# Gathering the first expert's rows in the router's stage, with VectorE's and GpSimd's work around it put in another order

## The reference, cut to what matters

```python
def moe_swiglu(x, w_router, b_router, w1, w3, w2):
    ...
    logits = (xt @ w_router).astype(jnp.float32) + b_router.astype(jnp.float32)
    top_v, top_i = lax.top_k(logits, TOP_K)
    gates = jax.nn.softmax(top_v, axis=-1)
    dense_gate = jnp.sum(jax.nn.one_hot(top_i, N_EXPERTS, dtype=jnp.float32) * gates[..., None], axis=1)
    y = jnp.zeros_like(xt)
    for e in range(N_EXPERTS):
        y = y + dense_gate[:, e:e + 1].astype(x.dtype) * swiglu(xt, w1[e], w3[e], w2[e])
```

## Time and profile before

| | |
|---|---|
| time, median of 3 runs | 2537.49 us (2537.44 to 2538.87) |
| profiled execution: its own time | 2535.22 us |
| its span in the trace | 2533.3 us |
| PE, PEld busy | 2451.1 us (97%), 2023.4 us (80%) |
| DVE, ACT, POOL busy | 1753.3 us (69%), 1056.2 us (42%), 607.0 us (24%) |
| router's end to the first expert's first matmul | 1052.6 us to 1065.45 us |

### The profile page before, as it was taken

How to read it: one execution, slowest core, us unless ns; L and a number is a source line. 1 busy time by engine, 2 the same in 40 slices (tenths; PEclk the granted TensorE clock), 3 DMA queues, 4 the chain that set the end, 5 groups by cost and what they waited for, 6 DMA issues and landing times. The chain is left out here.

```text
span 2533.3 us, 40965 instructions
## 1 busy us (share of the span) xinstructions
PE 2451.1 (97%) x15775; PEld 2023.4 (80%) x15775; DVE 1753.3 (69%) x2889; ACT 1056.2 (42%) x1586; POOL 607.0 (24%) x495
## 2 busy tenths in 40 slices
PE   8999999999999999899999999999999999999998
PEld 6788887788887889799999999887676577767576
DVE  7945666468987757767666676674887666688567
ACT  4444323321221352555555455534444454244453
POOL 2404221430240331244233442340023000024001
PEclk9999999999999999899999999999999999999999
DMA  4321002336553757467777777844222213322121
GB/s 158 96 82 41 2 3 67 120 136 203 166 180 111 211 163 266 147 226 250 225 252 239 233 249 225 276 153 152 71 80 61 73 59 100 94 80 72 33 84 67
DMA packets 265197, 348.87 MB, mean 138 GB/s; under 512 B 23184, under 2 KB 221008, under 8 KB 264400
## 3 DMA queue, kind: packets, MB, share of 16 engines
q1 hardware_dynamic: 250272, 301.24, 36.8%
q0 software_dynamic: 9136, 30.28, 3.5%
q10 hardware_dynamic: 5632, 15.21, 1.8%
HBM read 323.37 MB, written 20.71 MB: 136 GB/s over the span
## 5 line engine op out<-in xcount | busy, mean ns | idle before, releaser
L3247 PE MATMUL ps<-x_feat_r,moe_w_hi 128*128 128x384 f32 x1408 | 405.2, 360 | 1.1 <-DVE x_feat_r L3359 1.1
L2754 DVE TENSOR_TENSOR moe_w_lo<-ring,moe_w_hi 128x2048 fp32r<-128x2048 f32 x144 | 315.4, 2191 | 128.5 <-ACT moe_w_hi L2749 128.4
L3250 PE MATMUL ps<-x_feat_r,moe_w_lo 128*128 128x192 f32 x1408 | 353.1, 251 | 0.0
L2749 ACT ACTIVATE moe_w_hi<-ring 128x2048 fp32r<-128x2048 f32 x144 | 254.9, 1770 | 95.1 <-PE ps L267 75.1
L3250 PEld LDWEIGHTS ps<-x_feat_r,moe_w_lo 128*128 128x128 f32 x1408 | 269.0, 191 | 0.3
L3247 PEld LDWEIGHTS ps<-x_feat_r,moe_w_hi 128*128 128x128 f32 x1408 | 264.3, 188 | 2.2 <-issue 1.9
L271 PE MATMUL ps<-x_free_r,ring_r 128*128 128x512 f32 x496 | 195.7, 395 | 0.0
L270 PE MATMUL ps<-ring_r,x_feat_r 128*128 128x256 f32 (+2 forms) x576 | 184.3, 320 | 0.0
L267 PE MATMUL ps<-x_feat_r,ffn_w_hi 128*128 128x512 f32 x352 | 139.3, 396 | 1.2 <-DVE ffn_w_lo L2697 1.2
L271 PE MATMUL ps<-x_feat_r,ffn_w_lo 128*128 128x512 f32 x352 | 139.4, 396 | 0.0
L270 PE MATMUL ps<-x_free_r,ffn_w_hi 128*128 128x512 f32 x352 | 138.5, 393 | 0.0
(11 more groups left out here) (676 smaller groups left out, 6448.5 us busy)
## 6 DMA issues: line engine op xcount, KB each, us to landing
ring<-in_moe_w SPq DMA_DIRECT2D x120, 1024.0 KB, 5.5
ring<-in_w_in SPq DMA_DIRECT2D x32, 1024.0 KB, 5.2
ring<-in_ffn_w SPq DMA_DIRECT2D x30, 1024.0 KB, 6.3
ring<-in_gdn_w_in SPq DMA_DIRECT2D x12, 1024.0 KB, 5.8
ring<-in_ada_t SPq DMA_DIRECT2D x24, 512.0 KB, 3.9
cond_w<-in_ada_t POOLq DMA_DIRECT2D x24, 512.0 KB, 6.2
ring<-in_moe_w SPq DMA_DIRECT2D x24, 512.0 KB, 3.8
ring<-in_s_w_glu SPq DMA_DIRECT2D x8, 1024.0 KB, 8.4
```

What stands on the lines that cost most here:

```text
L2749: self.prog.nc.scalar.activation(self.flat(self.hi, j % SPLITS, j), self.raw(j), ACT.Copy).then_inc(self.hi_done, 1)
L2754: self.prog.nc.vector.tensor_tensor(self.flat(self.lo, j % SPLITS, j), self.raw(j), self.flat(self.hi, j % SPLITS, j).bitcast(F32), ALU.su ...
L3247: mm = nc.tensor.matmul(out, wh[:, k, cs], both[:, k, :], start=(k == 0), stop=False)
L3250: mm = nc.tensor.matmul(out[:, 0:SLOTS], wl[:, k, cs], xg[0][:, k, :], start=False, stop=(k == KD - 1))
```

## The change

1. The two indirect DMAs of the first expert's rows are issued by GpSimd at the end of the router's stage, after `stored` and `spot_read`, into a buffer `moe_first_rows` that is allocated there and kept as `rows_in`. They no longer stand at the head of the experts' stage.
2. In the router's stage VectorE computes the flag before it reads `spot`, where it did so after.
3. In the experts' stage VectorE makes the first rows' low halves, `x_lo(0)`, between the first two `split_lo`, where it did so after both.
4. GpSimd's `acc = ALPHA * x_tok` waits until `x_lo(0)` is done.
5. TensorE's first `keep_busy` has four matmuls in place of five.

```diff
-        keep_busy(prog, 6, 5)
+        keep_busy(prog, 6, 4)
         turn(0, at_start=True)
         keep_busy(prog, 6, 4)
...
         S_.split_lo(dve, 0, 0)
+        x_lo(0)
         S_.split_lo(dve, 0, 1)
-        x_lo(0)
         low_gate, top_gate = find_homes()
...
+        pool.wait_ge(x_lo_done, 3)
         for t in range(NT):
             ins = nc.gpsimd.tensor_scalar(prog.acc[:, t, :], prog.x_tok[:, t, :], ALPHA, None, ALU.mult)
         ins.then_inc(acc_ready, 1)
...
-                    if i == 4:
-                        late = slice(0, SLOTS - P)
-                        for dst, at in ((rows_in[:, 0, :], spot[:, 0:1]), (rows_in[late, 1, :], spot[late, 1:2])):
-                            eng.indirect_dma_start(out=dst, out_offset=None, in_=prog.x_rows,
-                                                   in_offset=bass.IndirectOffsetOnAxis(ap=at, axis=0)
-                                                   ).then_inc(prog.first_rows, 16)
...
-                dve.wait_ge(spot_ready, 1)
-                nc.vector.tensor_copy(spot[:, 0:1], ps[:, 7, 0:1])
-                nc.vector.tensor_copy(spot[late, 1:2], ps[late, 7, 2:3]).then_inc(spot_read, 1)
                 dve.wait_ge(ranked, 2)
...
                 nc.vector.tensor_scalar(flag[:, :], den[:, 0:1], SLOTS + 0.5, None, ALU.is_lt)
+                dve.wait_ge(spot_ready, 1)
+                nc.vector.tensor_copy(spot[:, 0:1], ps[:, 7, 0:1])
+                nc.vector.tensor_copy(spot[late, 1:2], ps[late, 7, 2:3]).then_inc(spot_read, 1)
...
                 pool.wait_ge(stored, 16 * NT)
+                pool.wait_ge(spot_read, 1)
+                for dst, at in ((first_rows[:, 0, :], spot[:, 0:1]), (first_rows[late, 1, :], spot[late, 1:2])):
+                    pool.indirect_dma_start(out=dst, out_offset=None, in_=prog.x_rows,
+                                            in_offset=bass.IndirectOffsetOnAxis(ap=at, axis=0)).then_inc(prog.first_rows, 16)
```

More of the change, by code:

```diff
@@ L3549, in new @@
             return own.enter_context(prog.nc.sbuf_tensor(f"{name}_{n}", shape, dt))
-        pick, token, spot = gather
-        rows_in = new("rows_in", [P, 2, D], F32)[:, :, :]
+        pick, token, spot, rows_in = gather
+        new("rows_in", [P, 2, D], F32)
         buf = (rows_in, new("y", [P, 2, D], F32), new("moved", [P, D], F32),
@@ L3600, in router @@
     with ExitStack() as own:
+        first_rows = prog.sbuf("moe_first_rows", [P, 2, D], own)
         w = prog.sbuf("moe_wr", [P, KD, EXPERTS], own)
@@ L3635, in logits_back @@
             return ps[:, 4 + t, UP_COLS:UP_COLS + EXPERTS]
+        gather = gather + (first_rows[:, :, :],)
         with Stage(prog, "s5_glu") as st:
@@ L3647, in router @@
                 st.counter(n) for n in ("pick_ready", "token_ready", "spot_ready", "spot_read"))
-            pick, token, spot = gather
+            pick, token, spot, _ = gather
             row_landed, silu_row, cond_used = st.pool_counter("row_landed"), st.counter("silu_row"), st.counter("cond_used")
@@ L3937, in _ @@
                     nc.scalar.activation(e[:, t, :], logit[:, t, 0:EXPERTS], ACT.Exp, bias=neg[:, t:t + 1]).then_inc(exped, 1)
+    return gather
 def moe_layer(prog, inp):
@@ L3949, in moe_layer @@
         gather = pick[:, :, :], token[:, :, :], spot[:, :]
-        router(prog, inp, gates[:, :, 0:EXPERTS], place, chosen, flag, table, gather)
+        gather = router(prog, inp, gates[:, :, 0:EXPERTS], place, chosen, flag, table, gather)
         moe_experts(prog, "moe", (inp["moe_w1"][0], inp["moe_w3"][0], inp["moe_w2"][0]), gates, place,
```

## The result

The changed kernel takes 2543.06 us (median of 17 runs, 2540.16 to 2547.0); the kernel before took 2536.71 us in 17 runs beside it (2535.31 to 2539.54). The ratio of the runs is 1.0023, 95% interval 1.0017 to 1.003, so the change is slower; the medians lie 6.35 us apart, where +5.4 us and 2542.9 us were forecast. The profiled execution of the change took 2544.73 us with a span of 2542.7; that of before 2535.22 and 2533.3. They are 9.5 us apart, more than the medians. Two differences between these executions have to be kept out of the reading. In the trace after, everything ahead of the barrier came 1.05 us earlier (row numbers read at 1051.53, not 1052.58 as in the earlier trace rows). So from here on places around the barrier are given as a distance behind the end of the second cast of the row numbers, T0.

The account below looks back on a forecast made before the run. TensorE's start was bound by VectorE's `x_lo(0)`, its third tile by VectorE's add. A release 6.3 us later, carried through the reordered work, made the tile 5.4 us later: 2537.49 + 5.4 = 2542.9 us, range 2538.0 to 2546.0.

Parts of the forecast that it names:

- GpSimd's drain with the gather in flight: Router's end: the drain is charged in full and holds the barrier; +4.3 to +6.8 us, chance 0.58.
- The cheap drain: Rival at the router's end: drain of 0.06 to 2.1 us, only the issues cost; +1.1 to +3.2 us, chance 0.18.
- The barrier that does not move: Rival: GpSimd reports once the DMAs are queued, only VectorE's reordering acts; -1.0 us, at best -2.2, chance 0.08.
- first issue behind T0: Router's end: GpSimd starts its gather 0.3 us after the row numbers, at the far end 0.85.
- drain behind the last issue: Router's end: GpSimd's drain ends 4.3 us after its last gather issue, near ends 3.8 and 4.74.
- late clock: Rival behind the barrier: TensorE's clock stays low through filler, turning and second filler; +6.8 to +9 us, chance 0.13.
- turning: Experts' start: TensorE turns the gathered rows in 1.73 us, up to 1.7 more with a late clock.
- VectorE's wait ahead of `x_lo(0)`: Experts' start: after its first split VectorE waits about 1 us for ScalarE's `x_hi` copies.
- end of `x_lo(0)` to end of the add: First expert: VectorE's second split, `find_homes`, third split, `pick` and the add, without a pause, 10.4 us.
- third tile later than before: First expert: TensorE gets its third weight tile at 1080.05 against 1074.7, 5.4 us later.
- The 2.67: First expert: time in us of a VectorE split beside GpSimd's scaling, against 2.29 alone.
- The full block: Rival in the first expert: shared port makes two splits each wait for a scaling; 5.4 us later still, chance 0.03.

Follow-up runs that it names:

- f1: The changed kernel with VectorE's old order in the experts, five filler matmuls and the scaling at once, so the moved gather alone; 2543.72 us, 1.0016 to before.
- f2: The kernel before with everything of the change but the moved gather; 2536.47 us, ratio 0.999 to before.
- f8: f2 with `find_homes` put ahead of VectorE's first split, the gather behind the barrier; 2536.59 us, ratio 0.9988 to before.
- g4: f8 run once more, on another chip; 2535.11 us, ratio 0.9995 to before.
- e7: The changed kernel with GpSimd's scaling free to start at once, without the wait for `x_lo(0)`; 2541.68 us, ratio 1.001 to before.
- e5: The kernel before with one added plain 4 KB DMA from GpSimd at the router's end; 2540.36 us, ratio 1.0005 to before.
- g2: f8 with ScalarE waiting for the raw tiles' own landing, not SyncE, and three matmuls in the second filler; 2535.12 us, ratio 0.9994 to before.
- g3: The changed kernel with only the 128-row DMA ahead of the barrier, the 64-row one behind it; 2543.47 us, ratio 1.0029 to before.
- e4: The changed kernel with seven filler matmuls for TensorE at the end of the router's stage; 2542.66 us, ratio 1.0011 to before.

## Why the prediction was right

The forecast mechanism, GpSimd's drain with the gather in flight, is the one that decided: f1 has the loss, f2 has not. The cheap drain needed an end before 1057.5 on the clock of before; moved by the 1.05 us, it ended at 1060.4. The barrier that does not move would have released near T0 + 0.6; it was T0 + 8.3. What the trace gives for each term:

| term | forecast | profile of the change |
|---|---|---|
| first issue behind T0 | 0.3 (far end 0.85) | 0.84 |
| the two issues | 2.26 | 2.26 |
| drain behind the last issue | 4.3 (3.8 to 4.74) | 4.72 |
| from the drain to the release | 0.05 | 0.45 |
| release later than before, by T0 | 6.3 (5.6 to 7.3) | 7.7 |
| ScalarE behind the release | 2.9 | 2.9 |
| eight filler matmuls | 4.5 (late clock 5.4) | 5.48 |
| turning | 1.73 | 2.1 |
| VectorE's wait ahead of `x_lo(0)` | 1.0 | 2.15 |
| end of `x_lo(0)` to end of the add | 10.4 | 11.1 |
| TensorE's wait for the third tile | 1.0 | 1.5 |
| third tile later than before | 5.4 | 8.5 by T0, 7.5 in the trace |

The first four rows are off by 1.4 us together, all in one direction. I had chosen the near value of the start from the gap ahead of other DMAs of GpSimd; the right row was the 0.85 us from a release to the first issue, since in both GpSimd had been waiting. The drain came at the end given by the indirect DMAs in the earlier trace rows to within 0.02 us, though the rows moved are fewer. The 0.45 us lie between GpSimd's two events: the first stands at 1059.4, directly behind its drain, and the second together with SyncE's release at 1059.8. In before's router stage the two are 0.1 us apart. It is not bound to GpSimd's drain being the last: at before's end of the experts' stage VectorE's drain ended last, at 1707.3, and the events stand at 1707.4 and 1707.8 all the same. Why the step is short in some stages and long in others stays open.

The rows of the late clock belong to a rival that the prediction had set apart, so the trace is that of the forecast and a part of this rival together. In the profiled execution it took its full price on the filler and 0.4 on the turning, but was over by then: +8.5 by T0, inside the +6.8 to +9 of that rival. Its reason, the longer pause, fell with f2, f8 and g4. It is a variation that before's executions may show as well, and so it is no part of the median's difference as far as could be seen.

VectorE's part was nearly right in total (11.1 against 10.4) and wrong in its pieces. The second split took 2.28 and not 2.67, the third 2.29; in exchange `find_homes` took 4.5 and not 3.65, `pick` 1.8 and not 1.0. That the pieces come out even is luck. The 2.67 was the mean of two unlike splits: in before's trace the first took 2.29 and the second 3.12, so "both slow down by a little" was a reading of a mean. The full block had priced 5.4 us for VectorE; VectorE lost 2.4 in all, 1.7 more than in e7. The Trainium skill (SBUF — State Buffer, section Terms, "shared port pair") says that the pair is held for the full instruction and that the loser fully blocks. For GpSimd the trace agrees: a scaling that starts into a split ends 2.6 to 2.7 us behind it, about a scaling's own 2.77. For VectorE it does not: the split at 1077.65 starts in the middle of a scaling (1075.81 to 1078.56) and still takes 2.29, and the longest loss of one of its instructions was 0.83 us. I had held the rule against the wrong engine.

The profiles put the third tile 7.5 to 8.5 us later and the medians 6.35. Part of the gap may be that before's one profiled execution had short clears (1.8 us), while three of the other five with an early release (e5, f2 and f8, not g2 and g4) show 3.1 to 3.6. In before's order VectorE works without a pause from ScalarE's first high half on, so there, unlike in f2, a late ScalarE would move the third tile; if before often has long clears, its usual third tile is later than 22.1. The runs don't show how often, so this stays open. That the sum of 5.4 came so near to 6.35 owes something to this: against its own trace the sum was 2 to 3 us short.

## What to carry to other kernels

Ahead of a barrier, a DMA issued from GpSimd's queue costs its issue, and the drain behind it, even if nobody in this stage needs the data: here 8.3 us behind the row numbers in place of 0.6, to hide a landing that was already hidden behind SyncE's handover of the weights. Before an issue is moved up, look at which engine drains last at the next barrier, and at what that drain cost behind the same kind of DMA elsewhere in the trace; and look for work that needs neither the rows nor the weights to fill the gap instead (`find_homes` there took away TensorE's wait for the third tile, though the time did not show it). When work of GpSimd is put off, look at what VectorE does at the later place: the scaling cost VectorE 0.65 us while that stood idle for much of the time; beside a busy VectorE it took 4.4 us more of GpSimd's time and 1.7 more of VectorE's.

## What the runs showed of the hardware

- GpSimd's drain is not free: 2.09 us with nothing in flight in a stage where it had issued DMAs (2.27 behind a finished gather), 2.18 behind a 4 KB DMA, 4.5 to 4.8 behind a gather's last issue. The earlier trace rows have 0.06 in a stage's end behind arithmetic.
- The release comes a further 0.1 to 0.5 us behind the last drain (0.17 in g3, 0.45 in the change, 0.5 at before's end of the experts' stage).
- A GpSimd scaling of 2.77 us that starts while a VectorE split runs ends 2.6 to 2.7 us behind that split (4.74, 4.0 and 4.4 us in the change). A split that starts 1.8 us into a scaling takes its usual 2.29; so does one that starts 1.0 us into one (e7). One that starts 0.24 us into a scaling takes 2.94 (e7), and before's second split, beside a scaling that had itself run into the first split, 3.12.
- SyncE's 31 clears take 1.8 us in some executions and 3.1 to 3.6 in others, the longest single one 321 to 713 ns where 25 to 30 is usual. ScalarE's start moves with them. The cause is open.
- The granted clock stood at 1.00 over 2 us in which TensorE did nothing and at 0.50 over 2 us behind it in which it was busy (e4). In the change it was still 0.50 for the first 5 us of filler and 1.00 at 1068, 7 us behind the filler's start.
